# A two-model forward pass on one Trainium2 core: an internal transfer goes to another queue, a small chain goes later, and four gate blocks change PSUM banks

## What is computed

```
hn   = rms_norm(h, attn_norm[0])
proj = hn @ w_in                      # (512,1024) @ (1024,4096)
q, f, i, g = split(proj, 4)           # 1024 columns each
lb     = lower_bounds                 # cumsum(softmax) - softmax[0]
forget = lb + (1 - lb) * sigmoid(f);  k = (1 - lb) * sigmoid(-f)
o = chunked recurrence over q, k, i, log(forget)
o = rms_norm(o) * gate_norm * silu(g) ;  out = o @ w_out
...
bias = rel_bias[t5_causal_bucket(rel)]   # DSA's bias, by distance and head
```

## Time and profile before

| | us |
|---|---|
| median of 3 runs (2801.51 to 2802.49) | 2801.8 |
| the profiled execution's own time | 2804.07 |
| its span | 2802.3 |
| PE busy in the span | 2741.4 (98%) |
| DVE, ACT, POOL busy | 1739.8, 1030.4, 120.8 |
| mean granted TensorE clock | 0.989 |

### The profile page before, as it was taken

How to read it: one execution, slowest core, us unless ns; L and a number is a source line. 1 busy time by engine, 2 the same in 40 slices (tenths; PEclk the granted TensorE clock), 3 DMA queues, 4 the chain that set the end, 5 groups by cost and what they waited for, 6 DMA issues and landing times.

```text
span 2802.3 us, 35578 instructions
## 1 busy us (share of the span) xinstructions
PE 2741.4 (98%) x14468; PEld 2228.1 (80%) x14468; DVE 1739.8 (62%) x2558; ACT 1030.4 (37%) x1502; POOL 120.8 (4%) x163
## 2 busy tenths in 40 slices
PE   7999899999999999999899999999999999999999
PEld 6788788888876688888776688888888788888887
DVE  4278757575667567474656657574664888653434
ACT  3245534242334544242435643232342222432322
POOL 0000000000014300000002300000000000000000
PEclk9999999999999999999999999999999999999999
DMA  6711034343323034343320036454432110333221
GB/s 164 159 54 46 31 108 157 115 151 102 76 88 100 27 111 157 127 135 105 87 84 31 1 102 211 150 180 136 139 103 72 35 34 16 121 111 100 91 83 53
DMA packets 262378, 276.84 MB, mean 99 GB/s; under 512 B 23559, under 2 KB 230919, under 8 KB 262216
## 3 DMA queue, kind: packets, MB, share of 16 engines
q1 hardware_dynamic: 232024, 219.51, 25.6%
q10 hardware_dynamic: 30192, 55.05, 6.1%
HBM read 267.19 MB, written 7.34 MB: 98 GB/s over the span
## 4 chain that ended last, share of the span: by engine, by line
PE 90%; DVE 4%; ACT 2%; DMA 2%; issue 1%; SPq 1%; ACTq 0%; DVEq 0%; POOL 0%
PE ps L571 25%; PE ps L573 24%; PE ps L572 24%; PE ps L1269 3%; PE ps L1301 2%; PE ps L883 2%; PE ps L1028 2%; DMA sb<-in_hgrn_w_in 1%; PE ps L1226 1%; PE ps L1045 1%; PE ps L1247 1%; SPq L2768 1%; PE ps L1062 1%; PE ps L1134 1%; PE ps L629 1%
## 5 line engine op out<-in xcount | busy, mean ns | idle before, releaser
L571 PE MATMUL ps<-sb 128*128 128x512 f32 (+2 forms) x3460 | 1293.2, 374 | 25.6 <-DVE sb L1957 6.2
L573 PE MATMUL ps<-sb 128*128 128x512 f32 (+2 forms) x3460 | 1273.4, 368 | 0.0
L572 PE MATMUL ps<-sb 128*128 128x512 f32 (+2 forms) x3460 | 1273.3, 368 | 0.0
L571 PEld LDWEIGHTS ps<-sb 128*128 128x128 f32 (+1 forms) x3460 | 654.9, 189 | 155.7 <-issue 38.0
L573 PEld LDWEIGHTS ps<-sb 128*128 128x128 f32 (+1 forms) x3460 | 654.7, 189 | 111.7
L572 PEld LDWEIGHTS ps<-sb 128*128 128x128 f32 (+1 forms) x3460 | 655.2, 189 | 108.1 <-issue 1.6
L1948 DVE TENSOR_TENSOR sb<-sb 128x2048 fp32r<-128x2048 f32 (+1 forms) x189 | 422.5, 2235 | 344.1 <-ACT sb L1387 344.1
L1387 ACT ACTIVATE sb<-sb 128x2048 fp32r<-128x2048 f32 (+2 forms) x196 | 365.0, 1862 | 293.1 <-PE ps L573 272.5
L2231 DVE SCALAR_TENSOR_TENSOR sb<-ps,sb 128x511 f32<-128x511 f32 (+1 forms) x264 | 193.6, 747 | 126.8 <-ACT sb L1635 121.6
L1635 ACT ACTIVATE sb<-ps,sb 128x512 f32<-128x512 f32 x132 | 96.0, 777 | 273.9 <-PE ps L573 270.8
L2266 DVE SCALAR_TENSOR_TENSOR sb<-sb 128x512 f32<-128x512 f32 x168 | 126.0, 750 | 12.5
(11 more groups left out here) (233 smaller groups left out, 2183.1 us busy)
## 6 DMA issues: line engine op xcount, KB each, us to landing
sb<-in_ffn_w_up SPq DMA_DIRECT2D x88, 1024.0 KB, 5.0
sb<-in_ada_w ACTq DMA_DIRECT2D x192, 256.0 KB, 3.1
sb<-in_ffn_w_down SPq DMA_DIRECT2D x32, 1024.0 KB, 5.1
sb<-in_ffn_w_down SPq DMA_DIRECT2D x16, 768.0 KB, 4.6
sb<-in_hy_w_in SPq DMA_DIRECT2D x12, 1024.0 KB, 5.3
sb<-in_hgrn_w_in SPq DMA_DIRECT2D x8, 1024.0 KB, 11.7
sb<-in_hgrn_w_in SPq DMA_DIRECT2D x16, 512.0 KB, 5.4
sb<-in_dsa_w_in SPq DMA_DIRECT2D x6, 1024.0 KB, 5.1
```

Of the source, the lines that this page charges most:

```text
L571: pe.matmul(o, al, bh, start=f, stop=False, **kw)
L572: pe.matmul(o, ah, bl, start=False, stop=False, **kw)
L573: m = pe.matmul(o, ah, bh, start=False, stop=l, **kw)
```

## The change

1. The transfer of `bv` to `scratch` leaves SP's program and is issued by ACT at the end of its `begin`, behind the last square of x. It goes by ACT's queue.
2. The lower bounds' chain is moved. ACT does its exponential ahead of the copies of `i` 2 and no longer ahead of those of `i` 0. DVE's part comes behind `split_low(4)` (the low half split off in `ahead` of `i` 1) and no longer ahead of `split_low(3)`. Behind the exponential ACT gets one dummy sigmoid on one element, which has the sigmoid table loaded there.
3. Gate blocks 0 and 2 use banks 0 and 1; blocks 1 and 3 use banks 2 and 3.

```diff
@@ PE, hgrn
-  project("pe_hgrn", ("hgrn", "g", c), (0, 1) if c % 2 else (2, 3), ...
+  project("pe_hgrn", ("hgrn", "g", c), (2, 3) if c % 2 else (0, 1), ...
@@ ACT, begin (behind the loop over j)
+  act.wait_ge(*at("bias", 0))
+  act.wait_ge(*at("bias", 1))
+  act.dma_start(scratch.ap(), bv[:, :].unsqueeze(1).broadcast_to([16, 128, 640])).then_inc(...)
@@ ACT, hgrn
   fence("begin")
-  act.wait_ge(*at("lb", 0))
-  act.activation(lbt[:, 1, :], lbt[:, 0, :], ACTF.Exp).then_inc(*mark("act_hgrn", ("lb", 1)))
   for c in range(4):
+      if c == 2:
+          act.wait_ge(*at("lb", 0))
+          act.activation(lbt[:, 1, :], lbt[:, 0, :], ACTF.Exp).then_inc(*mark("act_hgrn", ("lb", 1)))
+          act.activation(warm[:, :], eps[:, :], ACTF.Sigmoid).then_inc(*mark("act_stat"))
       for tt in range(4):
...
-  j, b = 2 * c + i, ((0, 1) if c % 2 else (2, 3))[i]
+  j, b = 2 * c + i, ((2, 3) if c % 2 else (0, 1))[i]
@@ DVE, hgrn
   split_low(2)
-  (lb 0, lb 2, lb 3, lb 4, lb 5: five small instructions)
   for c in range(4):
       ahead(("hgrn", "i", c))
+      if c == 1:
+          (the same five)
...
-  j, b = 2 * c + i, ((0, 1) if c % 2 else (2, 3))[i]
+  j, b = 2 * c + i, ((2, 3) if c % 2 else (0, 1))[i]
@@ SP
   weights(0, NRAW + NW)
-  sp.wait_ge(*at("bias", 0))
-  sp.wait_ge(*at("bias", 1))
-  load("scratch", scratch.ap(), bv[:, :].unsqueeze(1).broadcast_to([16, 128, 640]))
   fence("begin")
   load("masks", H.masks[:, :], A["c_masks"])
```

More of the change, by code:

```diff
@@ L856, in hgrn @@
                 for c in range(4):
-                    project("pe_hgrn", ("hgrn", "g", c), (0, 1) if c % 2 else (2, 3), [("g_mm", 2 * c + i) for i in range(2)],
+                    project("pe_hgrn", ("hgrn", "g", c), (2, 3) if c % 2 else (0, 1), [("g_mm", 2 * c + i) for i in range(2)],
                             [[("g", 2 * c + i)] for i in range(2)], ready=ready)
@@ L1503, in begin @@
                         split(0)
+                act.wait_ge(*at("bias", 0))
+                act.wait_ge(*at("bias", 1))
+                act.dma_start(scratch.ap(), bv[:, :].unsqueeze(1).broadcast_to([16, 128, 640])).then_inc(*mark("ld_scratch", ("scratch",), by=16))
             def hgrn():
                 fence("begin")
-                act.wait_ge(*at("lb", 0))
-                act.activation(lbt[:, 1, :], lbt[:, 0, :], ACTF.Exp).then_inc(*mark("act_hgrn", ("lb", 1)))
                 for c in range(4):
+                    if c == 2:
+                        act.wait_ge(*at("lb", 0))
+                        act.activation(lbt[:, 1, :], lbt[:, 0, :], ACTF.Exp).then_inc(*mark("act_hgrn", ("lb", 1)))
+                        act.activation(warm[:, :], eps[:, :], ACTF.Sigmoid).then_inc(*mark("act_stat"))
                     for tt in range(4):
@@ L2117, in hgrn @@
                 split_low(2)
[L2118 to L2127, removed]
                 for c in range(4):
                     ahead(("hgrn", "i", c))
+                    if c == 1:
+                        lower = v("lower", 0, 8)
+                        dve.tensor_tensor(lbt[:, 0, :], lower, lower, SUB).then_inc(*mark("dve_hgrn", ("lb", 0)))
+                        dve.wait_ge(*at("lb", 1))
+                        dve.reciprocal(lbt[:, 0, :], lbt[:, 1, :]).then_inc(*mark("dve_hgrn", ("lb", 2)))
+                        dve.wait_ge(*at("lb", 2))
+                        dve.tensor_tensor(lbt[:, 1, :], lbt[:, 1, :], lbt[:, 0, :], MUL).then_inc(*mark("dve_hgrn", ("lb", 3)))
+                        dve.wait_ge(*at("lb", 3))
+                        dve.tensor_tensor(lbt[:, 2, :], lbt[:, 1, :], lbt[:, 1, :], SUB).then_inc(*mark("dve_hgrn", ("lb", 4)))
+                        dve.wait_ge(*at("lb", 4))
+                        dve.tensor_scalar(lbt[:, 3, :], lbt[:, 2, :], -1.0, 1.0, MUL, ADD).then_inc(*mark("dve_hgrn", ("lb", 5)))
                 for c in range(4):
                     for i in range(2):
-                        j, b = 2 * c + i, ((0, 1) if c % 2 else (2, 3))[i]
+                        j, b = 2 * c + i, ((2, 3) if c % 2 else (0, 1))[i]
                         dve.wait_ge(*at("sg", j))
```

## The result

The change makes the kernel slower: 2813.0 us median of five runs (2809.7 to 2814.6) against 2801.8 (2801.5 to 2802.5) on the same chip. The ratio is 1.0036, 95% interval 1.0025 to 1.0047. The profiled execution took 2812.3 us, with a span of 2810.5. That is 8.2 above the profiled execution of before. I compare the traces with each other, and the medians with each other.

What follows compares the result with a forecast made beforehand. PE was taken as the bound, busy for 2741.4 of 2802.3 us. Late `i` 3 +12.2, clock +2.5 and gains -6.9 gave +7.8: 2811.9 profiled, median 2809.6, range 2798 to 2817.

Steps and rivals of the forecast that it cites:

- Transfer in the way: Weight loads in the dense part: the 49 us bias transfer hinders them; an item beside it takes 25.6 us.
- Item 3 is requested at 24.92 as before and starts at 26.0: SP's queue: item 3 starts beside the bias transfer at 26.0, ends at 51.6 and lands at 52.4, hidden.
- The turns: SP's and ACT's queues: one packet from each in turn, whatever their length; 0.40 us per weight packet.
- The gap's place: PE: `i` 2 starts at 56.0, then some 15 us idle ahead of `i` 3, released by ACT's copies.
- rival 3: SP held too: item 3 starts at 39.9, `i` 2 at 69.5, `i` 3 at 85.2; +7.1, median 2808.9; chance 0.13.
- Late `i` 3: PE at `i` 3: starts at 83.35 where it was 71.17, 12.2 us late.
- Clock: PE behind the 15 us gap ahead of `i` 3: low clock costs 2.5 us, bounds 1.6 and 4.
- head start: PE at `g` 0: it needs only the first two copies of `i` 3, a gain of 0.7 us.
- `g` blocks: Ahead of `g` 2 and head 0: gains of 2.8 and 0.15, clock 1.6, freed banks 1.65 us.
- The chain's 5.5 us of the stall: ACT behind item 4: the lower bounds' chain takes 5.5 of 7.4 us before the copies of `i` 2.
- `i` 1's 2.9 us: PE at `i` 1: with the chain moved it starts at 43.7 where it was 46.59, a gain of 2.9.
- Heads: From head 0 on: the heads run as before, only shifted.

Runs made afterwards that it cites:

- the first experiment: Only the bias transfer moved to ACT's queue, chain and banks as before, against the kernel before: 2812.6 us, ratio 1.0037.
- The kernel with half the copies: Changed kernel with 64 of the 128 copies on ACT's queue, the other 64 made later DRAM to DRAM on SP's queue: 2793.3 us, 0.9968.
- the pieces alone: Kernel before with only the bias transfer cut into eight requests of 16 copies between the weights on SP's queue: 2800.3 us, 0.9994.
- the three together: Changed kernel's chain and banks, bias transfer in eight requests of 16 copies between the weights on SP's queue: 2793.5 us, 0.9967.

## Why the prediction was right, and where it wasn't

The direction and the size held. 2813.0 lies in the range of 2798 to 2817, 3.4 us above the predicted 2809.6. Of these, 3.0 is the 2.3 and 0.7 by which the profiled executions stand off their medians; in the profiled time the forecast was 2811.9 and 2812.3 was measured. That closeness is in part luck: the terms were off both ways, and the two traces start `i` 0 almost 1 us apart.

- **Transfer in the way.** Right, and shown by the first experiment: alone it costs 10.4 us.
- **"Item 3 is requested at 24.92 as before and starts at 26.0": the step that failed.** It was requested at 23.95, but its first packet moved at 36.6 and only 4 packets before 38. The turns were right (782 to 783 packets), but they begin only when some 14 us of what lies in the other queue has gone. Rows 11 and 12 could not show this: they are stretches of work that had been under way.
- **The gap's place.** From that step came a single gap of 15 us ahead of `i` 3. In fact 14.96 us lie ahead of `i` 2 and 3.17 ahead of `i` 3. This is the timetable of rival 3, to a fraction of a us: `i` 2 at 69.03 (69.5 worked out), `i` 3 at 85.19 (85.2), 14.0 us late. So close a match is luck: counted from `i` 0, `i` 3 is 15.0 late. Its mechanism is not what happened: it had SP held at item 3's request, and that took 0.37 us. I had the right effect there and gave it 0.13, since I knew only one way to it.
- **Late `i` 3.** +14.0 measured for +12.2.
- **Clock.** 1.7 us fell behind `i` 3's start; 1.4 more, behind `i` 2's start, is within the 14.0. My 2.5 was for one gap. From `i` 3 to `g` 0 it was 13.07 us for 12.57 before: +0.5, where clock less head start were to give 2.5 - 0.7 = +1.8. The kernel with half the copies, at full clock there, took 11.58: so the clock cost 1.5 and the head start was worth 1.0.
- **`g` blocks.** From `g` 0 to head 0: 43.60 us for 49.91, -6.3, where 2.8 + 0.15 + 1.6 + 1.65 = 6.2 was worked out. The sum: +14.0 + 0.5 - 6.3 = +8.2, as the traces show (141.86 to 133.65). The 1.6 for the clock is the least certain term: with the banks alone, a gap of 2.89 us at the same place left the clock up.
- **The chain's 5.5 us of the stall.** 4.1 between split and copies in the trace, 2.7 by the experiment that leaves it in its place, some 4 up to head 0 with the clock.
- **Gains that don't add up.** The prediction treats `i` 1's 2.9 us as a gain of its own. It is one only if the weights come earlier as well: the chain alone gave +3.9, chain and banks -0.1, the pieces alone -1.7, the three together -8.8. A gap taken away ahead of a fixed arrival turns up again at the arrival.
- **Heads.** Unchanged to 0.1 us between these two traces, as forecast; that close is luck, since the kernels above differ there by up to 2.6 us.

By the Trainium skill (DMA: Bandwidth & Descriptors, Queues, rings and completion order) an engine drains a whole packet of typically 9 to 17 descriptors from one ring before it switches. The trace agrees that the engines alternate between queues, 782 to 783, but the units are of 1 KB and 2.56 KB each, and the first 13.5 us show no alternation at all.

## What to carry to other kernels

Moving a slow transfer to another issuing engine doesn't move it out of the way of the weights. The queues share the same 16 engines, what was queued first on one may go ahead of the other for some 14 us, and after that a short packet waits for each long one; cut the slow transfer into pieces and place them between the urgent loads, or make it smaller. Before counting a gap ahead of a late transfer as a gain, ask whether the transfer comes earlier too. When a timetable rests on the moment at which a second queue starts, look for a row in which it starts from empty.

## What the hardware showed that I had not expected

- A weight item landed 41.9 us after its request and not 5.4, though SP's issue of it took 0.37 us. The first packets waited until 11.7 us (32 copies), 13.6 us (64 copies in short packets), 15.3 us (64 copies) and 13.3 to 14.3 us (128 copies in one request) of the other queue had moved; with 8 copies they moved 1.3 us behind the request.
- The bias transfer seems to be bound by its source, which is argued and not shown. 2.6 MB from 16 partitions took 27.4 us, the last 11 of them beside item 3; the copy of as many bytes from DRAM to DRAM landed in 11.9 us, but in packets of 41 KB. Packets of half the length left the rate of the slow one nearly as it was (1.39 MB for 1.44 in 14 us).
- A gap of 3.46 us ahead of `i` 1 left the clock up, one of 3.21 us at the same place was followed by 5.7 us at 0.51. With gaps of 3.84 or 3.85 us there, the 5.7 us behind ran at 0.50 (transfer alone), 0.50 (transfer and banks) and 0.76 (banks alone). So one trace doesn't price the clock behind a short gap.
